# Scores of the second block as three float32r passes over high and low parts, two heads from two partition halves

## The reference

```python
q, k = rms_norm(q, q_g), rms_norm(k, k_g)          # head dimension 64
q, k = axial_rope(q, ang), axial_rope(k, ang)      # kinds A and C only
logits = einsum("bqhd,bkhd->bhqk", q, k) * 64 ** -0.5
p = softmax(logits)                                # tokens see context and tokens, context sees context
```

## Time and profile before

| | us |
|---|---|
| time, median of three | 2571.68 (2567.77, 2571.68, 2584.24) |
| span of the profiled execution, first to last instruction | 2584.9 |
| TensorE busy | 2324.4 (90%) |
| VectorE busy | 1492.0 (58%) |
| ScalarE busy | 1010.7 (39%) |
| GpSimd busy | 845.5 (33%) |

### The profile page before, as it was taken

The page is one execution under the profiler, slowest core; times in us unless marked ns, Lnnn a source line. Parts: engine busy times, 40 slices in busy tenths (PEclk is TensorE's granted clock), DMA queues, the critical chain, the costliest instruction groups (busy, mean ns, idle before and its releaser), DMA issues.

```text
span 2584.9 us, 39576 instructions
## 1 busy us (share of the span) xinstructions
PE 2324.4 (90%) x14736; PEld 1939.2 (75%) x14736; DVE 1492.0 (58%) x2854; ACT 1010.7 (39%) x1843; POOL 845.5 (33%) x544
## 2 busy tenths in 40 slices
PE   6969888999798889899999998999999888879898
PEld 5968788989687888777777785777778555667677
DVE  4594479645944787346663215556323788842565
ACT  3434356443343554443332324332234433224332
POOL 2445333124453331043332123342313433232443
PEclk8989889999898999989999999999999899989998
DMA  6433544554334445431113322112332111123111
GB/s 210 139 97 108 156 147 155 180 155 145 92 112 157 146 144 178 130 121 33 33 35 115 113 90 62 61 58 57 99 98 84 55 41 33 50 90 114 58 58 58
DMA packets 72848, 262.92 MB, mean 102 GB/s; under 512 B 8032, under 2 KB 10208, under 8 KB 72416
## 3 DMA queue, kind: packets, MB, share of 16 engines
q1 hardware_dynamic: 71392, 256.31, 31.4%
q0 software_dynamic: 1280, 4.20, 0.5%
HBM read 259.43 MB, written 1.05 MB: 101 GB/s over the span
## 4 chain that ended last, share of the span: by engine, by line
PE 63%; DVE 24%; issue 5%; ACT 4%; POOL 2%; DMA 2%; ACTq 0%; DVEq 0%; SPq 0%; POOLq 0%
PE gemm L397 12%; PE gemm L399 10%; PE gemm L398 10%; PE gemm L645 6%; PE gemm L435 5%; PE score L684 5%; DVE r L1239 3%; PE obank L716 3%; PE tbank L614 3%; DVE w_lo L292 3%; DVE d L1329 2%; DVE d L1185 2%; PE stat L625 1%; PE obank L720 1%; DMA ring<-wall 1%
## 5 line engine op out<-in xcount | busy, mean ns | idle before, releaser
L292 POOL TENSOR_TENSOR w_lo<-ring,w_hi 128x1024 fp32r<-128x1024 f32 x208 | 508.7, 2449 | 629.8 <-ACT w_hi L829 628.8
L397 PE MATMUL gemm<-g_hi,w_hi 128*128 128x256 f32 x1344 | 404.7, 301 | 72.6 <-DVE w_lo L292 40.5
L829 ACT ACTIVATE w_hi<-ring 128x1024 fp32r<-128x1024 f32 x344 | 362.4, 1054 | 105.9 <-PE gemm L399 34.9
L397 PE MATMUL gemm<-h_hi,w_hi 128*128 128x512 f32 (+1 forms) x928 | 387.4, 417 | 13.8 <-DVE h_lo L1551 8.4
L398 PE MATMUL gemm<-g_lo,w_hi 128*128 128x256 f32 x1344 | 393.4, 293 | 0.0
L399 PE MATMUL gemm<-g_hi,w_lo 128*128 128x256 f32 x1344 | 392.6, 292 | 0.0
L398 PE MATMUL gemm<-h_lo,w_hi 128*128 128x512 f32 (+1 forms) x928 | 352.5, 380 | 0.0
L399 PE MATMUL gemm<-h_hi,w_lo 128*128 128x512 f32 (+1 forms) x928 | 352.2, 380 | 0.0
L397 PEld LDWEIGHTS gemm<-g_hi,w_hi 128*128 128x128 f32 x1344 | 274.6, 204 | 91.5 <-DVE w_lo L292 44.8
L1096 ACT ACTIVATE pr<-score,small 128x512 f32<-128x512 f32 (+1 forms) x192 | 128.1, 669 | 464.9 <-DVE small L1448 464.9
L397 PEld LDWEIGHTS gemm<-h_hi,w_hi 128*128 128x128 f32 x928 | 179.6, 194 | 149.7 <-issue 110.6
(11 more groups left out here) (266 smaller groups left out, 4016.4 us busy)
## 6 DMA issues: line engine op xcount, KB each, us to landing
ring<-wall SPq DMA_DIRECT2D x478, 512.0 KB, 3.7
r<-nbias POOLq DMA_DIRECT2D x16, 256.0 KB, 3.0
cst<-consts SPq DMA_DIRECT2D x1, 2340.5 KB, 10.3
r<-x_t SPq DMA_DIRECT2D x1, 1024.0 KB, 4.9
x<-ctx_t SPq DMA_DIRECT2D x1, 1024.0 KB, 15.5
y_t<-x SPq DMA_DIRECT2D x4, 256.0 KB, 2.3
d<-pos SPq DMA_DIRECT2D x1, 128.0 KB, 10.2
```

The lines of the kernel that those rows point to most:

```text
L292: eng.tensor_tensor(w_lo[:, q % SPLITS, :, :], ring[:, t % RING, :, :], w_hi[:, q % SPLITS, :, :].bitcast(F), ALU.subtract)\
L397: pe.matmul(out, w[0][:, k, :], x[0], start=start, stop=False)
L829: act.activation(w_hi[:, q % SPLITS, :, :], ring[:, t % RING, :, :], ACT.Copy).then_inc(S["hi_ready"], 1)
```

## The change

Each score becomes three float32r passes, q high by k high, q low by k high, q high by k low, summed in the bank. One call of `scores` now does the two halves of a query tile, pass by pass in turn: pass 1 of half 0, pass 1 of half 1, pass 2 of half 0, and so on, each half in its own bank. So:

- `units` has the order of C (tile, then half) in all layers, `scores` and `biggest` run at even units for two units, and `scores` waits for the exponentials of both units before.
- ScalarE rounds q (`q_split_hi`, at the last unit behind `roped`; in B behind the evacuation, from `raw`) and k (`k_split_hi`, in A both chunks ahead of the loop, in B and C chunk by chunk after unit 1).
- VectorE makes the low part of q (`q_split_lo`) at the last unit behind `q_rms`; in B this takes the place of the copy of q. `scores` waits for it (`q_split`) instead of `roped`.
- GpSimd makes the low part of k over k itself (`k_split_lo`): ahead of the loop between `q_side` and `q_pow`, and in B and C at the start of each head for the next one. `scores` waits for `k_split`.
- `r1`, `d1` and `rot` are allocated earlier so that the high and low parts can lie over them.

```diff
                 def scores(c, u):
-                    t, a = us[u][0], HD * us[u][1]
+
+                    t = us[u][0]
                     kc = c // 4 if kind == "A" else c
                     s = n["s"]
                     wait_scores_read(pe, s - 2)
+                    wait_scores_read(pe, s - 1)
                     if u == 0:
-                        pe.wait_ge(S["roped"], rbase(L) + nk + c + 1)
-                    bk = sbk[s % 2]
-                    q = qT[a:a + HD, c % 2, :]
-                    if t < 2:
-                        ins = pe.matmul(bk[:, :], q[:, t * P:(t + 1) * P], kT[a:a + HD, kc, :], start=True, stop=True)
-                    else:
-                        pe.matmul(bk[:, 0:C], q[:, 2 * P:3 * P], kT[a:a + HD, kc, T:N2], start=True, stop=True)
-                        ins = pe.matmul(bk[:, C:2 * C], q[:, 3 * P:4 * P], kT[a:a + HD, kc, T:N2], start=True, stop=True)
-                    ins.then_inc(S["s_ready"], 1)
-                    n["s"] += 1
+                        pe.wait_ge(S["q_split"], L * KC + c + 1)
+                        pe.wait_ge(S["k_split"], kbase(L) + (nk if kind == "A" else c + 1))
+                    banks = (sbk[s % 2], sbk[(s + 1) % 2])
+                    kh = k_high(kind)[:, kc % 2, :]
+                    kl = k_lo[:, kc, :]
+                    qh, ql = q_hi[:, c % 2, :], q_lo[:, c % 2, :]
+                    parts = ((qh, kh), (ql, kh), (qh, kl))
+                    blocks = ((t, 0, 0, N2),) if t < 2 else ((2, 0, T, C), (3, C, T, C))
+                    for tile_, to, at, w in blocks:
+                        for i, (q, k) in enumerate(parts):
+                            for hh in range(2):
+                                a = HD * hh
+                                ins = pe.matmul(banks[hh][:, to:to + w], q[a:a + HD, tile_ * P:(tile_ + 1) * P], k[a:a + HD, at:at + w],
+                                                start=(i == 0), stop=(i == 2))
+                                if i == 2 and tile_ == blocks[-1][0]:
+                                    ins.then_inc(S["s_ready"], 1)
+                    n["s"] += 2
...
                     for u in range(NU):
-                        scores(c, u)
+                        if u % 2 == 0:
+                            scores(c, u)
...
+                def k_split_hi(j):
+
+                    act.activation(k_high(kind)[:, j % 2, :], kT[:, j, :], ACT.Copy).then_inc(S["k_hi_ready"], 1)
+
+                def q_split_hi(c):
+
+                    R = rbase(L) + nk + c
+                    if kind == "B":
+                        src = raw[:, R % 2, 0:NQ]
+                    else:
+                        act.wait_ge(S["roped"], R + 1)
+                        src = qT[:, c % 2, 0:NQ]
+                    act.activation(q_hi[:, c % 2, 0:NQ], src, ACT.Copy).then_inc(S["q_hi_ready"], 1)
...
+                for j in range(2 if kind == "A" else 1):
+                    k_split_hi(j)
                 evac_z(0)
+                if kind != "B":
+                    q_split_hi(0)
...
+                        if u == 1 and kind != "A" and c + 1 < KC:
+                            k_split_hi(c + 1)
                         if u == NU // 2 and c + 1 < KC:
                             evac_q(c + 1)
+                        if u == NU - 1 and kind != "B" and c + 1 < KC:
+                            q_split_hi(c + 1)
...
+                def q_split_lo(c):
+
+                    R = rbase(L) + nk + c
+                    dve.wait_ge(S["q_hi_ready"], L * KC + c + 1)
+                    src = raw[:, R % 2, 0:NQ] if kind == "B" else qT[:, c % 2, 0:NQ]
+                    ins = dve.tensor_tensor(q_lo[:, c % 2, 0:NQ], src, q_hi[:, c % 2, 0:NQ].bitcast(F), ALU.subtract)
...
                     for u in range(NU):
-                        biggest(c, u)
+                        if u % 2 == 0:
+                            biggest(c, u)
+                            biggest(c, u + 1)
                         if u == NU - 1 and c + 1 < KC:
                             q_end(c + 1)
...
                         if u == NU - 1 and c + 1 < KC:
                             q_rms(c + 1)
+                            q_split_lo(c + 1)
...
+                def k_split_lo(j):
+
+                    pool.wait_ge(S["k_hi_ready"], kbase(L) + j + 1)
+                    pool.tensor_tensor(k_lo[:, j, :], kT[:, j, :], k_high(kind)[:, j % 2, :].bitcast(F), ALU.subtract).then_inc(S["k_split"], 1)
+
                 q_side(0)
+                for j in range(2 if kind == "A" else 1):
+                    k_split_lo(j)
                 q_pow(0)
                 for c in range(KC):
+                    if kind != "A" and c + 1 < KC:
+                        k_split_lo(c + 1)
                     split_to(AT["qz", L] + 2 * c + 1 + AHEAD)
```

More of the change, by code:

```diff
@@ L160, in build_program @@
         assert arena_at % 32 == 0
+        r1 = sb("r1", [P, KC, T])
+        r1_at = nc.sbuf_base - 4 * KC * T
+        d1 = sb("d1", [P, KC, T])
+        d1_at = nc.sbuf_base - 4 * KC * T
+        rot = sb("rot", [P, 2, N2])
+        rot_at = nc.sbuf_base - 4 * 2 * N2
+        assert r1_at % 32 == 0 and d1_at % 32 == 0 and rot_at % 32 == 0
         def split_buffer(name, shape, col):
@@ L192, in build_program @@
         cos1 = arena[:, 15872:16128]; sin1 = arena[:, 16128:16384]
-        r1 = sb("r1", [P, KC, T])
-        d1 = sb("d1", [P, KC, T])
         sq = sb("sq", [P, 4, N2])
@@ L203, in build_program @@
         shf = sb("shf", [P, 2, N2])
-        rot = sb("rot", [P, 2, N2])
         pt = sb("pt", [P, 2, N2])
@@ L218, in build_program @@
         qT = d1[:, 4:8, :].rearrange("p (s a) t -> p s (a t)", s=2)
+        q_hi = nc.alloc_sbuf_tensor_at("q_hi", [P, 2, N2], FR, offset=d1_at)
+        q_lo = nc.alloc_sbuf_tensor_at("q_lo", [P, 2, N2], FR, offset=d1_at + 4 * 4 * T)
+        k_hi_r = nc.alloc_sbuf_tensor_at("k_hi_r", [P, 2, N2], FR, offset=r1_at)
+        k_hi_b = nc.alloc_sbuf_tensor_at("k_hi_b", [P, 2, N2], FR, offset=rot_at)
+        k_lo = nc.alloc_sbuf_tensor_at("k_lo", [P, KC, N2], FR, offset=arena_at + 4 * 8192)
         W1 = TAPS - 1 + T
@@ L278, in build_program @@
             k_sq ss_ready rk_ready q_sq qss_ready qss_read rq_ready z_evac zs_ready gated_ready comb_ready
-            oss_ready ors_ready osb_ready nb_used v_ready k_used lam_sum lam_exp gs_ready yo_evac yo_used st_read""".split()
+            oss_ready ors_ready osb_ready nb_used v_ready k_used lam_sum lam_exp gs_ready yo_evac yo_used st_read
+            q_hi_ready q_split k_hi_ready k_split""".split()
         S = {n: sem(n) for n in names}
@@ L297, in units, with k_high @@
         def units(kind, need_ctx):
[L299 to L302, removed]
+            return [(t, m) for t in ((0, 1, 2) if need_ctx else (0, 1)) for m in range(2)]
+        def k_high(kind):
+            return k_hi_b if kind == "B" else k_hi_r
         def lag(kind):
@@ L1058, in block2 @@
                         rk(j - 1)
+                def k_split_hi(j):
[8 more added lines that the diff above has]
+                    act.activation(q_hi[:, c % 2, 0:NQ], src, ACT.Copy).then_inc(S["q_hi_ready"], 1)
                 def evac_q(c):
                     evac_qk(rbase(L) + nk + c, sq[:, 2 + c % 2, 0:NQ], cc(f"qg{L}"), S["q_sq"], NQ)
+                    if kind == "B":
+                        q_split_hi(c)
                 def evac_z(c):
@@ L1383, in block2, with plain_qk @@
                         .then_inc(S["ada_gate"], 1)
-                def plain_qk(R, N, dst, scale=None):
+                def plain_qk(R, N, dst, scale):
                     dve.wait_ge(S["raw_ready"], R + 1)
-                    if scale is None:
-                        ins = dve.tensor_copy(dst, raw[:, R % 2, 0:N])
-                    else:
-                        ins = dve.tensor_tensor(dst, raw[:, R % 2, 0:N], scale, ALU.mult)
-                    seq(ins)
+                    seq(dve.tensor_tensor(dst, raw[:, R % 2, 0:N], scale, ALU.mult))
                     dve.sem_inc(S["roped"], 1)
@@ L1411, in q_end @@
                 def q_end(c):
-                    R, dst = rbase(L) + nk + c, qT[:, c % 2, 0:NQ]
+                    if kind != "B":
+                        rope_end(rbase(L) + nk + c, NQ, qT[:, c % 2, 0:NQ])
+                def q_split_lo(c):
[3 more added lines that the diff above has]
+                    ins = dve.tensor_tensor(q_lo[:, c % 2, 0:NQ], src, q_hi[:, c % 2, 0:NQ].bitcast(F), ALU.subtract)
                     if kind == "B":
-                        plain_qk(R, NQ, dst)
+                        seq(ins)
+                        dve.sem_inc(S["roped"], 1)
+                        dve.sem_inc(S["raw_used"], 1)
+                        dve.sem_inc(S["q_split"], 1)
                     else:
-                        rope_end(R, NQ, dst)
+                        ins.then_inc(S["q_split"], 1)
                 def q_rms(c):
@@ L1555, in block2 @@
                 q_rms(0)
+                q_split_lo(0)
```

## The result

The changed kernel took 2599.39 us (median of 7 runs, 2584.53 to 2605.16) against 2574.55 for the kernel before (7 runs on the same chip): ratio 1.0076, 95% interval 1.0058 to 1.0094. The forecast was 2558, 0.5% faster; the time lies inside the range 2522 to 2610, on the other side of no change.

What follows compares the result with a forecast made beforehand. TensorE, busy 90% of the span, was taken to bound the kernel, in C in turns with VectorE. A -6, B -16, C +4, last A -3 and prologues +8 gave -13 us, 2558, range 2522 to 2610.

Steps and rivals of the forecast that it cites:

- Passes at once: Score pairs on TensorE: both heads' passes run side by side, 0.70 us a pair; one after the other would be 1.40.
- The context pair: Context scores on TensorE: 12 short passes, 1.26 to 1.38 us; running at once gains nearly nothing there.
- The saving, 4.2 us a head: TensorE's score work in a six-unit head: 7.5 us before, 3.3 after, so 4.2 saved.
- The gaps: TensorE's idle before a head's first score: 3.3 us in A, 1.6 in B, over 4 in C, 2.7 in last A.
- The question whether GpSimd's power holds it: VectorE's new subtraction at the head boundary: taken as not held, 0; if held, 1.65 us more a boundary.
- The prologues: Before each layer's loop: VectorE's subtraction waits for GpSimd's two k subtractions; +2 us a layer, +8 in all.
- The clock in A and last A, taken at 1.00: TensorE's granted clock in these layers' heads: expected to stay 1.00 despite boundary gaps of 3.3 and 2.7 us.
- rival 2: Boundary gaps in A and last A lower TensorE's clock: 1.7 us a head, +24, 2582 with passes at once; chance 0.2.
- C, +0.9 us a head: Layer C's heads: 1.5 us kept in TensorE's part, 2.4 added in VectorE's part; +0.9 a head, +4 the layer.
- B, -1.7 us a head: Layer B's heads: 4.2 us saved, 2.5 added by the boundary gap and waiting transposes; -1.7 a head, -16 the layer.
- Rival 1: Score pairs on TensorE: the two heads' passes go one after the other; 2596 us, chance 0.2.
- Rival 3: Head boundaries: the added tail is covered by more room in TensorE's queue or VectorE's order; 2503 us, chance 0.13.

Runs made afterwards that it cites:

- q early: Changed kernel with the next head's q chain moved one unit earlier on ScalarE and VectorE; 2533.5 us, ratio 0.9796 to 0.9883 to the kernel before.
- Gemm first: Changed kernel with one piece of the next projection issued ahead of a head's first scores, from the second head on; 2572.8 us.
- the kernel with the passes apart: Changed kernel with projection products over all 128 rows issued between one head's three passes and the other's; 2714.0 us.
- float32 pairs: Changed kernel's order and pairs, but each score one float32 product with no split of q or k; 2558.6 us, 0.9917 of the kernel before.

## Why the prediction was wrong

The direction was. Step by step:

- **Passes at once** ("I take at once"): right. A pair takes 0.89 us to the next gemm product, where the forecast had 0.70; apart, one head alone takes 0.85. The Trainium skill, "TensorE: Matmul & The Clock Gate", Part 3 (The mechanism), has matmuls in distinct row groups start some ns apart; the runs agree (0.89 us for both halves, 0.85 for one). The context pair, put at 1.26 to 1.38, takes no more than 0.91 (1224.93 to 1225.84): its halves overlap as well, which the step denied.
- **The saving, 4.2 us a head**: 3.5 measured (TensorE busy in a B head at full clock, 27.64 before and 24.11 after; 3.7 in A), mis-sized by 0.5 to 0.7. The terms for the scores themselves come out: before 1.05 and 0.43 for the gemm product behind, as charged, and after, in the chain, 0.88 for a full pair and 0.91 for a context pair with 0.43 behind, 3.3 us a head as forecast, though by two errors that cancel (the full pair 0.2 dearer, the context pair 0.35 cheaper). What the sum left out are the places from which a score has gone: directly behind the product with v, a gemm product takes 0.28 to 0.34 in the chain and not 0.23 (B heads at full clock). The rest of the 0.5 to 0.7 stays open.
- **The gaps**: right to 0.2. 3.2 for 3.3 in A, 1.6 for 1.6 in B, 4.4 for "over 4" in C, 2.5 for 2.7 in last A. VectorE's subtraction takes 0.68 at the median for 0.7. The question whether GpSimd's power holds it didn't arise: in every steady head the subtraction starts 0.05 to 0.16 us ahead of the power, which in A, B and C now takes 2.02 to 2.14 us for 1.65. The prologues: A's first score waits 8.0 us for 5.2, C's 8.0 for 6.6, last A's 8.7 for 6.1, B's 3.3 for 1.9: 8.2 more in all, for "+8". In three of the four they wait for k's low part:

```profile
1150.10 0.80 PE L706 MATMUL score<-k_hi_r,q_hi 64*128 64x512 f32 x2 [8.01 <-POOL k_lo L1843]
```

- **The clock in A and last A, taken at 1.00**: this is the step that failed. It was rival 2, with 0.2 and a price of 1.7 us a head, +24. In A's six heads the granted clock was 0.89 to 0.94, in last A's 0.83 to 1.00. Its price is read from TensorE's busy time, as the work is the same: 26.2 us a head in A on the mean, 24.0 at full clock (q early); 15.5 in last A, 14.1 in the one head that kept it. That is 2.2 + 1.3 = 3.5, and 24 us over seven heads of each, rival 2's price. Gemm first, with the longest wait cut to 1.6, gave 20 us back, some 13 of them by the clock. The steps between the second and the eighth sums lie 10.7 us over the forecast in A and 6.8 in last A; the rest of the two layers came out 4.5 and 1.2 better than forecast, which is why the table of layers has 6.3 and 5.7. The forecast took a gap of 3.06 us in the first block, with 1.00 behind it, as the nearer row; but it was one row of one place, and behind B's 1.6 the clock fell in some heads and not in others. So the length of the gap alone does not decide it, and a row of another stage is no bound. At full clock A would be 24.0 busy + 3.5 of waits = 27.5 us, or 28.05 as measured with the gap filled: the 27.9 of the forecast. The Trainium skill, same page, "HAM oscillation", has a loop that waits once in each pass pay for the clock each time; the granted clock agrees in eleven of the twelve heads of A and last A and in two of the six of B. It would have been a reason to give this rival more than 0.2.
- **C, +0.9 us a head**: +2.5 measured (33.09 for 30.61), of which the pairing is 1.0 and the split at the boundary 1.5; the early chain takes it back to 30.8. The sign was right, the size too small by 1.6 a head (by the layer's length, 6 us). What the clock, 0.79 to 0.92 in these heads, has to do with it is not shown.
- **B, -1.7 us a head**: -0.9 where the clock held (of the 0.8 that are missing 0.7 is the saving above), and 28.2 us, 0.6 more than before, in the two heads of six where it didn't.

Rival 1 is excluded by the kernel with the passes apart. Rival 3 (the boundary covered, 2503) was wrong as a forecast, yet moving the q chain one unit gave much of what it asks for: 2533 us. That the time lies inside the stated range is owed to the rivals that the range takes in, not to the forecast, which by itself had 2540 to 2575.

## What to carry to other kernels

Before you price a cheaper form of an operation, price the new arrangement with the old form: here issuing two heads' 64-row products next to each other gave 3.15 of the 3.7 us a head, and the cheaper passes 0.55, less than the chain of splits that they need. Work taken off the bounding engine becomes a wait at the first place where a side chain is late, so move that chain in the same change; each alone gave under 1%, both 2.5%. And where a loop stands still once a turn on TensorE, count its clock as lost until rows of that same loop show it kept: waits of 1.6 and 1.2 us cost less than one of 3.2.

## What was not expected of the hardware

- Two float32 products of 64 rows in the two halves run at once as well: four records in 1.06 us, one head alone 1.05.
- Their order in the queue matters little: three passes of one half and then three of the other still ran side by side, in 0.89 us. Only a product over all 128 rows between them parted them (0.85 each).
- The clock fell behind gaps of 1.6 us in some heads and held in others of the same layer (B's steps of 28.2 and 26.75 us, granted clock 0.94 and 1.00).
- With nearly the same idle time in an A head, 3.5 and 3.4 us, the clock was under 1.00 in all six heads where 3.2 of it was one wait, and 1.00 in five of six where the longest was 1.8 (the changed kernel, float32 pairs).
- GpSimd's power over 8 columns, 1.65 us before, took 2.02 to 2.14 where VectorE's subtraction started 0.05 to 0.16 us ahead of it.
